# A chunked bidirectional recurrence: a masked copy over a prefilled negative identity, and another order of the work around it

## The chip, the cores and the metric

The kernel runs on one core of a Trainium2 chip. The metric is the device time of one execution in microseconds. It is shown as the median of three runs, and beside it one execution was taken with the hardware profiler.

## The reference

The program computes two model blocks, one after the other. The change lies in the second block, in its recurrence `wkv_scan`, which runs forward and backward over 1,280 tokens (256 of context, whose final states start the rest, then 1,024 of the sequence), with 8 heads of 64 columns:

```python
def wkv_scan(s0, r, w, k, v, a, b, reverse):
    def step(s, inp):
        r_t, w_t, k_t, v_t, a_t, b_t = inp
        sa = jnp.einsum('bhvk,bhk->bhv', s, a_t)
        s = s * w_t[:, :, None, :] + sa[..., :, None] * b_t[:, :, None, :] + v_t[..., :, None] * k_t[:, :, None, :]
        return s, jnp.einsum('bhvk,bhk->bhv', s, r_t)
```

It is called with `v` as it is, the decay as `w`, `-kk` as `a` and `kk * a` as `b`. Only the outputs of the sequence are used; of the context only the final states count.

## The kernel before, in words

`rwkv_chunks` (line 1974) computes the recurrence in `NCK` = 20 chunks of `CK` = 64 tokens, both directions at once (index `d`). Four of them are context. Within a chunk the step-by-step recurrence becomes a lower triangular system of 64 unknowns for each head and direction. Its matrix I + L is inverted by doubling: `x` holds the inverse of the diagonal blocks so far (of 2, 4, 8, ... tokens), and each of `LEVELS` = 5 levels makes blocks twice as large.

A level is a chain over three engines. TensorE multiplies `lm` (the lower matrix) by `x` in `products`, into PSUM tile `ps0`; VectorE masks the result to the level's blocks in `masked` (line 2212, into `t1`). Beside that TensorE transposes `x` in `x_turned`, and ScalarE copies the transpose to `xt` (line 2162). TensorE multiplies both in `advanced`, again into `ps0`, and VectorE adds that to `x` in VectorE's `advanced` (line 2218). At the last level TensorE forms the transposed result instead (line 2314, `rc_ps<-rc_xt,rc_t`), and VectorE adds it to `xt` (line 2288): the inverse.

Names of PSUM tiles are joined to `rc_ps` in the trace; a group is recognized by what it reads:

- `rc_x,rc_lm`: the product of a level (in the text P0 to P4); `all_ident,rc_x`: the transposes of x (four records); `rc_t,rc_xt`: the advance (A0 to A3). X0 to X3 are the updates of x on line 2218.
- `rc_ar,rc_bst` with 64x128 elements: the lower products of the next chunk (`lower`), from which VectorE makes `lm` (line 2224); `rc_bst,rc_ar`: the row product (`lower_rows`), from which `first` makes the start of `x`.
- `rc_ar,rc_kst`: the key product, from which VectorE makes `lk` (line 2267). `rc_v,rc_lk` and `rc_S,rc_ar`: the right side of the system (`right_side`, `right_side_of_state`); `rc_g,rc_xt` and `rc_gs,rc_xt`: `solved`; `rc_lm,rc_u`, `rc_lk,rc_v` and `rc_ar,rc_S`: `outputs` and `outputs_of_state`; `rc_u,rc_brows` and `rc_v,rc_krows`: `state`. `all_ident,rc_vst`: transposes of v.

The start of `x` for the next chunk is I - L on the first, smallest blocks:

```python
V.tensor_tensor(paired(b["x"][:, sl]), crossed(0, d), over(T.level[d][0][:]), ALU.mult)
V.tensor_tensor(paired(b["x"][:, sl]), paired(b["x"][:, sl]), over(T.ident2[:]), ALU.add)
```

These are lines 2230 and 2234, two instructions each (one per direction).

GpSimd forms the factors `bst`, `kst` and `ar` of the chunk after (lines 2092 to 2116) and copies v (line 2125). VectorE adds the outputs to `y` in `outputs` (lines 2244 and 2247, four instructions in a chunk), sums up the state in `summed` (line 2253) and scales it in `advance_state` (line 2260).

Each engine runs its own instructions strictly in the order in which `body` writes them down; semaphores hold an instruction until its operands are there. TensorE's order is written out for all 20 chunks, the other engines loop over the later ones two at a time. In `body(i)` TensorE works on the inverse of chunk i, and between its levels on the solution, the outputs and the state of chunk i - 1. Bodies 0 to 4 form no outputs. Double buffers are chosen by `sl`.

## Time and profile before

| | us |
|---|---|
| median of three runs | 3118.64 |
| lowest, highest | 3117.55, 3123.63 |
| the profiled execution | 3105.69 |
| its span in the profile | 3103.9 |
| TensorE matmuls busy | 2486.0 |
| VectorE busy | 1704.7 |
| ScalarE busy | 964.7 |
| GpSimd busy | 630.0 |

The profiled execution took 12.95 us less than the median of the three runs. The span begins with the first and ends with the last recorded instruction; 1.8 us of the execution lie around it. Busy time is a mean over stages that differ much: the recurrence is one stage of them, and only what its own rows say holds for it. TensorE works on 32-bit data in several passes, so the trace has two matmul records for each matmul of the program, and 32 records for a product. A timeline row joins neighbouring instructions of one kind: its first number is the start of the first, its second the time until the last one's result. In brackets stands how long the engine had idled, and on what it had waited; "issue" is a time in which it waited for nothing that the profile shows.

### The profile page before, as it was taken

The page shows a single profiled execution, that of the slowest core. Times are in us where ns is not written, and L with a number is a line of the kernel's source. Part 1 is how long each engine was busy: PE and PEld are TensorE (multiplying, and loading weights), DVE is VectorE, ACT ScalarE, POOL GpSimd, SP SyncE. Part 2 cuts the span into 40 slices and gives each one's busy share as a digit, 9 for nine tenths or more (in the row PEclk, how much of TensorE's full clock was granted, in tenths as well). Part 3 has the DMA queues.
Part 4 walks back from the last instruction along what each step waited for, and adds up shares of the span by engine and source line. Part 5 has one row for each costly group of instructions (what it writes and reads, how often), then busy time and mean ns, then how long its engine had stood idle before and what let it go on. Part 6 is the DMA issues. An engine that isn't in the chain of part 4 may idle for free. (4 is left out here: it accounts for less than half of the span.)

```text
span 3103.9 us, 57059 instructions
## 1 busy us (share of the span) xinstructions
PE 2486.0 (80%) x23774; PEld 1915.1 (62%) x23774; DVE 1704.7 (55%) x2130; ACT 964.7 (31%) x1492; POOL 630.0 (20%) x618
## 2 busy tenths in 40 slices
PE   4698998879989299997667777773575689999993
PEld 1586655447657278885256666661365678888882
DVE  2792448421124412664645555556435589999993
ACT  2111441210021400012333333320102067777772
POOL 0231457112200033220054444410000010001000
PEclk8899999989999599996589999996785589999997
DMA  9132004321122212110411011101434089999994
GB/s 379 71 126 87 1 1 146 92 102 34 51 85 85 86 58 68 41 35 16 170 28 26 20 24 24 24 4 48 166 104 176 0 326 409 398 399 389 398 385 151
DMA packets 132709, 405.57 MB, mean 131 GB/s; under 512 B 55082, under 2 KB 64938, under 8 KB 102674
## 3 DMA queue, kind: packets, MB, share of 16 engines
q1 hardware_dynamic: 119252, 359.52, 30.8%
q0 software_dynamic: 4608, 16.78, 2.2%
q10 hardware_dynamic: 8640, 26.19, 2.2%
q8 instruction: 168, 2.75, 0.4%
q14 instruction: 41, 0.34, 0.0%
HBM read 346.83 MB, written 55.61 MB: 130 GB/s over the span
## 5 line engine op out<-in xcount | busy, mean ns | idle before, releaser
L2927 DVE TENSOR_TENSOR ex_wl<-ew_raw,ex_wh 128x2048 fp32r<-128x2048 f32 x192 | 435.5, 2289 | 41.9 <-ACT ex_wh L2889 38.5
L2889 ACT ACTIVATE ex_wh<-ew_raw 128x2048 fp32r<-128x2048 f32 x192 | 367.5, 1919 | 217.0 <-PEq L89 109.3
L125 PE MATMUL sp_acc<-b2h_hi,sp_wh 128*128 128x512 f32 (+1 forms) x528 | 194.8, 369 | 11.8 <-POOL sp_wl L1614 11.8
L125 PE MATMUL sp_acc<-b2h_lo,sp_wh 128*128 128x512 f32 (+1 forms) x528 | 194.5, 368 | 0.0
L125 PE MATMUL sp_acc<-b2h_hi,sp_wl 128*128 128x512 f32 (+1 forms) x528 | 194.2, 368 | 0.0
L2162 ACT ACTIVATE rc_xt<-rc_ps 128x256 f32<-128x256 f32 x200 | 69.3, 391 | 229.1 <-PE rc_ps L2321 228.9
L2212 DVE TENSOR_TENSOR rc_t<-rc_ps,b_level 128x256 f32<-128x256 f32 x200 | 75.5, 419 | 103.4 <-PE rc_ps L2307 103.4
L1100 DVE TENSOR_TENSOR merge_sg<-b_pj,merge_sg 128x512 f32<-128x512 f32 x16 | 11.1, 692 | 217.8 <-ACT merge_sg L1086 217.8
L2810 POOL DMA_INDIRECT x<-ex_o,ex_at x16 | 26.5, 1656 | 490.8 <-DVE ex_o L2950 490.8
L125 PE MATMUL merge_acc<-merge_hh,merge_wh 128*128 128x512 f32 x256 | 101.5, 397 | 26.0 <-POOL merge_wl L119 20.7
L2798 POOL DMA_INDIRECT ex_xs<-h,ex_at x16 | 27.5, 1721 | 456.9 <-DVE ex_at L2952 434.2
L125 PEld LDWEIGHTS sp_acc<-b2h_hi,sp_wh 128*128 128x128 f32 x528 | 100.1, 190 | 28.6 <-POOL sp_wl L1614 12.2
L1612 POOL CAST sp_wh<-sp_w 128x1024 fp32r<-128x1024 f32 x26 | 27.1, 1042 | 434.8 <-DMA sp_w<-in_w_conv 251.2
L2307 PE MATMUL rc_ps<-rc_x,rc_lm 64*64 64x64 f32 x3200 | 73.5, 227 | 51.6 <-DVE rc_x L2234 50.0
L125 PEld LDWEIGHTS sp_acc<-b2h_hi,sp_wl 128*128 128x128 f32 x528 | 100.0, 189 | 16.7
L125 PEld LDWEIGHTS sp_acc<-b2h_lo,sp_wh 128*128 128x128 f32 x528 | 100.2, 190 | 16.4
L125 PE MATMUL pr_acc<-h_hi,pr_wh 128*128 128x512 f32 x224 | 89.6, 400 | 22.2 <-POOL pr_wl L205 20.6
L2831 PE MATMUL ex_G<-ex_wh,ex_xh 128*128 128x512 f32 x256 | 102.1, 399 | 1.4 <-DVE ex_xl L2932 1.4
L2307 PEld LDWEIGHTS rc_ps<-rc_x,rc_lm 64*64 64x64 f32 x3200 | 59.2, 136 | 68.1 <-issue 67.9
L2831 PE MATMUL ex_O<-ex_wh,ex_hh 128*128 128x512 f32 x256 | 99.7, 389 | 1.6 <-DVE ex_hl L2943 1.6
L2831 PE MATMUL ex_U<-ex_wh,ex_xh 128*128 128x512 f32 x256 | 100.9, 394 | 0.0
L2833 PE MATMUL ex_G<-ex_wh,ex_xl 128*128 128x512 f32 x256 | 100.7, 393 | 0.0
(459 smaller groups left out, 6379.3 us busy)
## 6 DMA issues: line engine op xcount, KB each, us to landing
ew_raw<-in_exp_gate SPq DMA_DIRECT2D x64, 1024.0 KB, 7.6
ew_raw<-in_exp_up SPq DMA_DIRECT2D x64, 1024.0 KB, 8.9
ew_raw<-in_exp_down SPq DMA_DIRECT2D x64, 1024.0 KB, 7.7
b_pj<-in_ada_w SPq DMA_DIRECT2D x24, 1024.0 KB, 18.4
rc_ac<-ac SPq DMA_DIRECT2D x40, 256.0 KB, 3.8
merge_w<-in_w_merge SPq DMA_DIRECT2D x16, 512.0 KB, 4.9
ac<-rp_ac SPq DMA_DIRECT2D x4, 2048.0 KB, 7.1
pr_w<-in_w_main SPq DMA_DIRECT2D x14, 512.0 KB
```

What stands on the lines that cost most here:

```text
L125: ins = nc.tensor.matmul(out, w[a][:, k, :], h[b][:, k, cols], start=(first and n == 0), stop=(last and n == 2))
L1100: nc.vector.tensor_tensor(sg[:, h, 0:1, :], merged[:, ds(b, 1), h * 512:(h + 1) * 512], sg[:, h, 0:1, :], ALU.mult).then_inc(weighed, 1)
L1612: nc.gpsimd.tensor_copy(wh[:, i % 2], w[:]).then_inc(q["w_rounded"], 1)
L2162: A.activation(dst(t[d]), src(d), ACT.Copy).then_inc(q[d][ready], 1)
L2212: V.tensor_tensor(paired(b["t1"][:]), crossed(0, d), over(T.level[d][l + 1][:]), ALU.mult).then_inc(s["t1_ready"], 1)
L2307: last = M(ps[n][c * CK:(c + 1) * CK, f, at:at + w], l(t[d])[k, h], r(t[d])[k, h], start=(i == 0), stop=(i == len(terms) - 1))
L2798: nc.gpsimd.indirect_dma_start(xs[:, m % 2, :], None, h_dram, bass.IndirectOffsetOnAxis(at[:, m:m + 1], 0)).then_inc(gathered[m % 2], 16)
L2810: nc.gpsimd.indirect_dma_start(x2, bass.IndirectOffsetOnAxis(at[:, x:x + 1], 0), o[:, x % 2, :], None, compute_op=ALU.add).then_inc(scatte ...
L2831: nc.tensor.matmul(acc[:, c], ah[:, k, :], wh[:, s, kk, c], start=(k == 0), stop=False)
L2833: last = nc.tensor.matmul(acc[:, c], al[:, k, :], wh[:, s, kk, c], start=False, stop=(k == KD - 1))
L2889: nc.scalar.activation(wh[:, n % RING], raw[:, n % RING], ACT.Copy).then_inc(q["w_hi"], 1)
L2927: V.tensor_tensor(wl[:, n % RING], raw[:, n % RING], wh[:, n % RING].bitcast(f32), ALU.subtract).then_inc(q["w_lo"], 1)
```

## The change

- VectorE's pair of multiplication and identity addition becomes one `copy_predicated` for each direction: where the mask of the first level is not zero it copies the row product over `x`, and elsewhere `x` stays. For that ScalarE fills `x` of the next chunk with minus the identity, between its third and fourth transposed copies. The first mask loses its sign. `x` now holds the negative of what it held; the updates on lines 2218 and 2288 become subtractions, and the solution is copied with the scale -1.
- TensorE: in the first level the transposes of x come ahead of `right_side`, and `right_side_of_state` and the advance ahead of the key product. `lower` of the next chunk moves ahead of the last level's transposes, and `lower_rows` ahead of its advance, with a wait for the last mask.
- VectorE: `lk` moves behind the first update of x, `outputs` ahead of the fourth mask, `summed` ahead of the fourth update, `lower` ahead of the last mask.

```diff
--- before.py
+++ after.py
...
@@ -2155,14 +2155,22 @@
                         hold(act, passed)
                         A.activation(b["e_end"][:, sl], b["last"], ACT.Copy).then_inc(s["kept"], 1)
 
-                def copy(done, count, dst, src, ready):
+                def copy(done, count, dst, src, ready, scale=1.0):
                     for d in range(2):
                         act.wait_ge(joint[done] if done in joint else q[d][done], count)
                         hold(act, passed)
-                        A.activation(dst(t[d]), src(d), ACT.Copy).then_inc(q[d][ready], 1)
+                        A.activation(dst(t[d]), src(d), ACT.Copy, scale=scale).then_inc(q[d][ready], 1)
 
                 def transposed(i, l, sl):
                     copy("xt_done", LEVELS * i + l + 1, lambda b: b["xt"][:, sl], lambda d: stayed(1, d), "xt_next")
+
+                def filled(c, sl):
+
+                    for d in range(2):
+                        if not (isinstance(c, int) and c < 2):
+                            act.wait_ge(joint["xi_done"], c - 1)
+                        hold(act, passed)
+                        A.activation(t[d]["x"][:, sl], spread(T.ident2[:], 1, HP), ACT.Copy, scale=-1.0).then_inc(q[d]["filled"], 1)
 
                 def right_side(count):
                     for d in range(2):
@@ -2180,7 +2188,7 @@
                         right_side(i)
                     transposed(i, 1, sl)
                     if old is not None:
-                        copy("u_done", i, lambda b: paired(b["u"][:]), lambda d: crossed(2, d), "u_ready")
+                        copy("u_done", i, lambda b: paired(b["u"][:]), lambda d: crossed(2, d), "u_ready", -1.0)
                     for d in range(2):
                         b, s = t[d], q[d]
                         act.wait_ge(s["rows_done"], i + 1)
@@ -2188,6 +2196,8 @@
                         A.activation(b["brows"][:, sl], stayed(3, d), ACT.Copy, scale=-1.0).then_inc(s["b_rows"], 1)
                         A.activation(b["krows"][:, sl], stayed(3, d, 1), ACT.Copy).then_inc(s["k_rows"], 1)
                     transposed(i, 2, sl)
+                    if following is not None:
+                        filled(i + 1, 1 - sl)
                     transposed(i, 3, sl)
                     transposed(i, 4, sl)
                     copy("v_done", i + 1, lambda b: b["v"][:], lambda d: stayed(3, d), "v_rows")
...
@@ -2215,7 +2226,7 @@
                     for d in range(2):
                         b, s = t[d], q[d]
                         dve.wait_ge(joint["xp_done"], (LEVELS - 1) * i + l + 1)
-                        V.tensor_tensor(paired(b["x"][:, sl]), crossed(0, d), paired(b["x"][:, sl]), ALU.add).then_inc(s["x_next"], 1)
+                        V.tensor_tensor(paired(b["x"][:, sl]), paired(b["x"][:, sl]), crossed(0, d), ALU.subtract).then_inc(s["x_next"], 1)
 
                 def lower(c, sl):
                     for d in range(2):
@@ -2227,11 +2238,9 @@
                     for d in range(2):
                         b, s = t[d], q[d]
                         dve.wait_ge(joint["pl_done"], c + 1)
-                        V.tensor_tensor(paired(b["x"][:, sl]), crossed(0, d), over(T.level[d][0][:]), ALU.mult).then_inc(s["x_ready"], 1)
-                    for d in range(2):
-                        b, s = t[d], q[d]
-                        dve.wait_ge(s["x_ready"], 2 * c + 1)
-                        V.tensor_tensor(paired(b["x"][:, sl]), paired(b["x"][:, sl]), over(T.ident2[:]), ALU.add).then_inc(s["x_ready"], 1)
+                        dve.wait_ge(s["filled"], c + 1)
+                        hold(dve, passed)
+                        V.copy_predicated(paired(b["x"][:, sl]), over(T.level[d][0][:].bitcast(u32)), crossed(0, d)).then_inc(s["x_ready"], 1)
 
                 def outputs(c):
                     for d in range(2):
@@ -2261,31 +2270,32 @@
 
                 def body(i, sl, half, old, here, following):
                     masked(i, 0)
+                    advanced(i, 0, sl)
                     for d in range(2):
                         b, s = t[d], q[d]
                         dve.wait_ge(joint["pk_done"], i + 1)
                         V.tensor_tensor(paired(b["lk"][:, sl]), crossed(3, d, 2 * CK), over(T.plus[d][:]), ALU.mult).then_inc(s["lk_ready"], 1)
-                    advanced(i, 0, sl)
                     masked(i, 1)
                     advanced(i, 1, sl)
                     masked(i, 2)
                     advanced(i, 2, sl)
-                    masked(i, 3)
                     if old == "all":
                         outputs(i - 1)
-                    advanced(i, 3, sl)
+                    masked(i, 3)
                     if old is not None:
                         summed(i)
+                    advanced(i, 3, sl)
+                    if following is not None:
+                        lower(i + 1, 1 - sl)
                     masked(i, 4)
                     if old is not None:
                         advance_state(1 - sl, i)
                     if following is not None:
-                        lower(i + 1, 1 - sl)
                         first(i + 1, 1 - sl)
                     for d in range(2):
                         b, s = t[d], q[d]
                         dve.wait_ge(joint["xi_done"], i + 1)
-                        V.tensor_tensor(b["xt"][:, sl], stayed(1, d), b["xt"][:, sl], ALU.add).then_inc(s["inverse"], 1)
+                        V.tensor_tensor(b["xt"][:, sl], b["xt"][:, sl], stayed(1, d), ALU.subtract).then_inc(s["inverse"], 1)
 
                 dve.wait_ge(cleared, 5)
                 lower(0, 0)
@@ -2327,13 +2337,16 @@
                     crossing(2, 2 * CK, (lambda b: b["bst"][:, sl], lambda b: b["ar"][:, sl])).then_inc(joint["pm_done"], 1)
 
                 def lower_rows(c, sl):
+                    if c:
+                        for d in range(2):
+                            pe.wait_ge(q[d]["t1_ready"], LEVELS * c)
                     crossing(0, CK, (lambda b: b["ar"][:, sl, :, 0:CK], lambda b: b["bst"][:, sl])).then_inc(joint["pl_done"], 1)
 
                 def products(i, l, sl):
                     for d in range(2):
                         if l == 0:
                             pe.wait_ge(q[d]["lm_ready"], i + 1)
-                            pe.wait_ge(q[d]["x_ready"], 2 * i + 2)
+                            pe.wait_ge(q[d]["x_ready"], i + 1)
                         else:
                             pe.wait_ge(q[d]["x_next"], (LEVELS - 1) * i + l)
                     crossing(0, CK, (lambda b: b["lm"][:, sl, :, 0:CK], lambda b: b["x"][:, sl])).then_inc(joint["t1_done"], 1)
@@ -2341,7 +2354,7 @@
                 def x_turned(i, l, sl):
                     for d in range(2):
                         if l == 0:
-                            pe.wait_ge(q[d]["x_ready"], 2 * i + 2)
+                            pe.wait_ge(q[d]["x_ready"], i + 1)
                             if i:
                                 pe.wait_ge(q[d]["inverse"], i)
                         else:
@@ -2394,15 +2407,14 @@
 
                 def body(i, sl, old, following):
                     products(i, 0, sl)
+                    x_turned(i, 0, sl)
                     if old is not None:
                         right_side(i, 1 - sl)
-                    x_turned(i, 0, sl)
+                        right_side_of_state(i, 1 - sl)
+                    advanced(i, 0, sl)
                     for d in range(2):
                         pe.wait_ge(q[d]["stk"], i + 1)
                     crossing(3, 2 * CK, (lambda b: b["kst"][:, sl], lambda b: b["ar"][:, sl])).then_inc(joint["pk_done"], 1)
-                    if old is not None:
-                        right_side_of_state(i, 1 - sl)
-                    advanced(i, 0, sl)
                     x_turned(i, 1, sl)
                     products(i, 1, sl)
                     if old is not None:
@@ -2427,14 +2439,14 @@
                     if old is not None:
                         state(i, 1 - sl)
                     advanced(i, 3, sl)
-                    x_turned(i, 4, sl)
-                    products(i, 4, sl)
                     if following:
                         if old == "all":
                             for d in range(2):
 
                                 pe.wait_ge(q[d]["y_added"], 2 * (i - CTX_CK) + 1)
                         lower(i + 1, 1 - sl)
+                    x_turned(i, 4, sl)
+                    products(i, 4, sl)
                     for d in range(2):
                         s = q[d]
                         if old is not None:
@@ -2446,9 +2458,9 @@
                         pe.wait_ge(s["v_staged"], i + 1)
                     for d in range(2):
                         turned(stayed(3, d), t[d]["vst"]).then_inc(q[d]["v_done"], 1)
-                    advanced(i, 4, sl)
                     if following:
                         lower_rows(i + 1, 1 - sl)
+                    advanced(i, 4, sl)
 
                 lower(0, 0)
                 lower_rows(0, 0)
@@ -3156,7 +3168,6 @@
     low = np.stack([(r // (2 * n) == c // (2 * n)) & (r // n > c // n) for n in (1, 2, 4, 8, 16, 32)]).astype(f)
     high = np.stack([(r // (2 * n) == c // (2 * n)) & (r // n < c // n) for n in (1, 2, 4, 8, 16, 32)]).astype(f)
     out["levels"] = np.stack([low, high])
-    out["levels"][:, 0] *= -1
     return {n: np.ascontiguousarray(a) for n, a in out.items()}
```

On TensorE, the start of a body that has outputs (P0 to the first transposes of the second level), before:

```order
L2307 MATMUL rc_ps<-rc_x,rc_lm 64x64 x16
L2307 MATMUL rc_ps<-rc_v,rc_lk 64x64 x16
L2321 MATMUL rc_ps<-all_ident,rc_x 128x128 x4
L2307 MATMUL rc_ps<-rc_ar,rc_kst 64x128 x16
L2314 MATMUL rc_ps<-rc_S,rc_ar 64x64 x16
L2307 MATMUL rc_ps<-rc_t,rc_xt 64x64 x16
L2321 MATMUL rc_ps<-all_ident,rc_x 128x128 x4
```

and now (line numbers are ten higher in the changed kernel):

```order
L2317 MATMUL rc_ps<-rc_x,rc_lm 64x64 x16
L2331 MATMUL rc_ps<-all_ident,rc_x 128x128 x4
L2317 MATMUL rc_ps<-rc_v,rc_lk 64x64 x16
L2324 MATMUL rc_ps<-rc_S,rc_ar 64x64 x16
L2317 MATMUL rc_ps<-rc_t,rc_xt 64x64 x16
L2317 MATMUL rc_ps<-rc_ar,rc_kst 64x128 x16
L2331 MATMUL rc_ps<-all_ident,rc_x 128x128 x4
```

The key product has moved from ahead of the first advance to behind it.

On TensorE, the end of such a body and the next chunk's first product, before:

```order
L2307 MATMUL rc_ps<-rc_t,rc_xt 64x64 x16
L2321 MATMUL rc_ps<-all_ident,rc_x 128x128 x4
L2307 MATMUL rc_ps<-rc_x,rc_lm 64x64 x16
L2307 MATMUL rc_ps<-rc_ar,rc_bst 64x128 x16
L2321 MATMUL rc_ps<-all_ident,rc_vst 128x128 x4
L2314 MATMUL rc_ps<-rc_xt,rc_t 64x64 x16
L2307 MATMUL rc_ps<-rc_bst,rc_ar 64x64 x16
L2307 MATMUL rc_ps<-rc_x,rc_lm 64x64 x16
```

and now:

```order
L2317 MATMUL rc_ps<-rc_t,rc_xt 64x64 x16
L2317 MATMUL rc_ps<-rc_ar,rc_bst 64x128 x16
L2331 MATMUL rc_ps<-all_ident,rc_x 128x128 x4
L2317 MATMUL rc_ps<-rc_x,rc_lm 64x64 x16
L2331 MATMUL rc_ps<-all_ident,rc_vst 128x128 x4
L2317 MATMUL rc_ps<-rc_bst,rc_ar 64x64 x16
L2324 MATMUL rc_ps<-rc_xt,rc_t 64x64 x16
L2317 MATMUL rc_ps<-rc_x,rc_lm 64x64 x16
```

The lower products stand ahead of the last transposes, and the row product ahead of the last advance.

On VectorE, the same stretch from the third update of x on, before:

```order
L2218 TENSOR_TENSOR rc_x<-rc_ps,rc_x 128x256 x2
...
L2212 TENSOR_TENSOR rc_t<-rc_ps,b_level 128x256 x2
...
L2244 TENSOR_TENSOR b2p_y<-rc_ps,b2p_y 128x4x64
...
L2247 TENSOR_TENSOR b2p_y<-rc_ps,b2p_y 128x4x64
...
L2218 TENSOR_TENSOR rc_x<-rc_ps,rc_x 128x256 x2
L2253 TENSOR_TENSOR rc_sum<-rc_ps,rc_S 128x256 x2
...
L2212 TENSOR_TENSOR rc_t<-rc_ps,b_level 128x256 x2
L2260 TENSOR_TENSOR rc_S<-rc_sum,rc_e_end 128x256 x2
...
L2224 TENSOR_TENSOR rc_lm<-rc_ps,b_minus 128x512 x2
L2230 TENSOR_TENSOR rc_x<-rc_ps,b_level 128x256 x2
...
L2234 TENSOR_TENSOR rc_x<-rc_x,b_ident 128x256 x2
L2288 TENSOR_TENSOR rc_xt<-rc_ps,rc_xt 128x256 x2
```

and now:

```order
L2229 TENSOR_TENSOR rc_x<-rc_x,rc_ps 128x256 x2
...
L2253 TENSOR_TENSOR b2p_y<-rc_ps,b2p_y 128x4x64
...
L2256 TENSOR_TENSOR b2p_y<-rc_ps,b2p_y 128x4x64
...
L2223 TENSOR_TENSOR rc_t<-rc_ps,b_level 128x256 x2
L2262 TENSOR_TENSOR rc_sum<-rc_ps,rc_S 128x256 x2
...
L2229 TENSOR_TENSOR rc_x<-rc_x,rc_ps 128x256 x2
...
L2235 TENSOR_TENSOR rc_lm<-rc_ps,b_minus 128x512 x2
...
L2223 TENSOR_TENSOR rc_t<-rc_ps,b_level 128x256 x2
L2269 TENSOR_TENSOR rc_S<-rc_sum,rc_e_end 128x256 x2
L2243 COPY_PREDICATED rc_x<-b_level,rc_ps 128x256 x2
L2298 TENSOR_TENSOR rc_xt<-rc_xt,rc_ps 128x256 x2
```

The output additions stand ahead of the fourth mask, the `lm` pair ahead of the last one, and one pair of masked copies stands where two pairs stood.

## Rows read from the trace of the kernel before

**Rows 1.** The page, its costliest groups: busy, mean ns, idle before and its releaser.

```profile
L2307 PE MATMUL rc_ps<-rc_x,rc_lm 64*64 64x64 f32 x3200 | 73.5, 227 | 51.6 <-DVE rc_x L2234 50.0
```

**Rows 2.** Windows, recurrence: us, busy PE, PEld, DVE, ACT, POOL, clock, DMA.

```profile
1562.00:2092.00 530.00, 402.62 (x14243) 347.67 (x14244) 293.02 (x696) 170.77 (x554) 221.79 (x345) 0.96 0.09 21
```

**Rows 3.** Timeline of DVE: start, us, line, op, count; three of twenty identity additions.

```profile
1566.71 1.35 DVE L2234 TENSOR_TENSOR rc_x<-rc_x,b_ident 128x256 f32<-128x256 f32 x2
...
1686.53 1.74 DVE L2234 TENSOR_TENSOR rc_x<-rc_x,b_ident 128x256 f32<-128x256 f32 x2
...
2060.80 0.75 DVE L2234 TENSOR_TENSOR rc_x<-rc_x,b_ident 128x256 f32<-128x256 f32 x2
```

**Rows 4.** Timeline of PE, one body without visible stalls.

```profile
1929.22 0.69 PE L2307 MATMUL rc_ps<-rc_x,rc_lm 64*64 64x64 f32 x32 [2.42 <-DVE rc_x L2234]
...
1930.90 1.10 PE L2307 MATMUL rc_ps<-rc_ar,rc_kst 64*64 64x128 f32 x32
...
1931.82 1.04 PE L2314 MATMUL rc_ps<-rc_S,rc_ar 64*64 64x64 f32 x30
...
1933.92 0.77 PE L2321 MATMUL rc_ps<-all_ident,rc_x 128*128 128x128 f32 x4 [0.53 <-DVE rc_x L2218]
...
1940.76 1.13 PE L2314 MATMUL rc_ps<-rc_ar,rc_S 64*64 64x64 f32 x32
...
1944.19 0.69 PE L2307 MATMUL rc_ps<-rc_t,rc_xt 64*64 64x64 f32 x32
...
1946.95 0.69 PE L2307 MATMUL rc_ps<-rc_x,rc_lm 64*64 64x64 f32 x32
...
1947.46 1.05 PE L2307 MATMUL rc_ps<-rc_ar,rc_bst 64*64 64x128 f32 x32
...
1949.04 1.09 PE L2314 MATMUL rc_ps<-rc_xt,rc_t 64*64 64x64 f32 x30
...
1950.02 0.63 PE L2307 MATMUL rc_ps<-rc_bst,rc_ar 64*64 64x64 f32 x30
...
1953.25 0.69 PE L2307 MATMUL rc_ps<-rc_x,rc_lm 64*64 64x64 f32 x32 [2.60 <-DVE rc_x L2234]
```

**Rows 5.** Timeline of DVE, the same body.

```profile
1932.08 1.29 DVE L2267 TENSOR_TENSOR rc_lk<-rc_ps,b_plus 128x512 f32<-128x512 f32 x2 [1.33 <-PE rc_ps L2307]
...
1943.18 0.76 DVE L2212 TENSOR_TENSOR rc_t<-rc_ps,b_level 128x256 f32<-128x256 f32 x2 [1.38 <-PE rc_ps L2307]
...
1945.78 0.75 DVE L2218 TENSOR_TENSOR rc_x<-rc_ps,rc_x 128x256 f32<-128x256 f32 x2
...
1947.72 0.76 DVE L2212 TENSOR_TENSOR rc_t<-rc_ps,b_level 128x256 f32<-128x256 f32 x2 [0.54 <-PE rc_ps L2307]
...
1948.39 0.75 DVE L2260 TENSOR_TENSOR rc_S<-rc_sum,rc_e_end 128x256 f32<-128x256 f32 x2
...
1950.70 0.76 DVE L2230 TENSOR_TENSOR rc_x<-rc_ps,b_level 128x256 f32<-128x256 f32 x2 [0.36 <-PE rc_ps L2307]
```

**Rows 6.** Timeline of POOL, the same body.

```profile
1942.21 1.33 POOL L2116 TENSOR_TENSOR rc_ar<-b2p_pT,rc_e 128x256 f32<-128x256 f32 x2 [3.12 <-PE rc_ps L2314]
...
1949.16 0.74 POOL L2125 COPY rc_vst<-b2p_pT 128x256 f32 x2 [5.61 <-PE rc_ps L2321]
```

**Rows 7.** Instructions of line 2234: ns min/median/max.

```profile
L2234 DVE TENSOR_TENSOR rc_x<-rc_x,b_ident x40: 416/831/985, 1566.7 to 2061.1; 128x256 f32<-128x256 f32 x40
```

**Rows 8.** Instructions of line 2517: ns min/median/max.

```profile
L2517 DVE RECIPROCAL ro_t<-ro_t x8: 3352/3353/3354, 2112.7 to 2189.6; 128x512 f32<-128x512 f32 x8
```

**Rows 9.** Timeline of ACT, between its third and fourth transposed copy.

```profile
1942.38 0.66 ACT L2162 ACTIVATE rc_xt<-rc_ps 128x256 f32<-128x256 f32 x2 [2.81 <-PE rc_ps L2321]
```

**Rows 10.** Timeline of PE, a body with stalls.

```profile
2017.67 0.27 PE L2307 MATMUL rc_ps<-rc_gs,rc_xt 64*64 64x64 f32 x1 [1.69 <-issue]
...
2021.97 0.21 PE L2307 MATMUL rc_ps<-rc_lk,rc_v 64*64 64x64 f32 x1 [0.59 <-issue]
```

**Rows 11.** DMA queues from 1686.53 to 2060.80: packets, MB, share.

```profile
q8 instruction: 83, 1.36, 1.5%
```

More of the change, by code:

```diff
@@ L1981, in rwkv_chunks @@
         ka = ph.sb("ka", [P, 2, HP])
-        names = ("decays", "kept", "stk", "v_staged", "rows_done", "v_done", "lm_ready", "x_ready",
+        names = ("decays", "kept", "stk", "v_staged", "rows_done", "v_done", "lm_ready", "filled", "x_ready",
                  "lk_ready", "b_rows", "k_rows", "v_rows", "t1_ready", "xt_done", "xt_next", "x_next", "inverse",
@@ L2198, in _ @@
                 decays(0, 0, 0)
+                filled(0, 0)
                 keep(0, 0)
@@ L2201, in _ @@
                 right_side(NCK)
-                copy("u_done", NCK, lambda b: paired(b["u"][:]), lambda d: crossed(2, d), "u_ready")
+                copy("u_done", NCK, lambda b: paired(b["u"][:]), lambda d: crossed(2, d), "u_ready", -1.0)
             @block.vector
```

## The prediction

> **What bounds the kernel now.** I read the page first. Its group of the recurrence's row products names the wait that matters: before those 3,200 matmuls TensorE sat idle for 51.6 us, nearly all of it until the identity addition on line 2234 had run [rows 1]. That is twenty waits of 2.5 us, one for each chunk. The windows view then gives the size of the stage: 530 us, in which TensorE's matmuls are busy 403 us, VectorE 293 us and everything else less, at a granted clock of 0.96 of the 2.4 GHz level [rows 2]. No engine is full; the stage is a chain that goes to and fro between TensorE and VectorE.
>
> The VectorE timeline gives the period. The identity addition comes at 1566.71 us (chunk 0), 1686.53 (chunk 5) and 2060.80 (chunk 19) [rows 3]. So bodies 0 to 4 take (1686.53 - 1566.71) / 5 = 23.96 us each, and bodies 5 to 18, which also form outputs, (2060.80 - 1686.53) / 14 = 26.73 us. One of the latter shows no stall of TensorE's own: 1929.22 to 1953.25, 24.03 us [rows 4]. I use it as the skeleton; the other 2.7 us are stalls that the views call "issue", such as 1.69 and 0.59 us in the middle of runs of matmuls that wait for nobody [rows 10].
>
> In the skeleton the reader should see three things. From the last but one advance (A3, 1944.19) to the next chunk's first product it takes 9.06 us, with two idle spots of TensorE in it, the last 2.60 us long [rows 4]. X3, VectorE's update of x after A3, starts at 1945.78, though A3's 0.69 us of data had ended at 1944.88: four output additions stood ahead of it [rows 4, 5]. And the end of the chunk is serial: row product (1950.02), mask (1950.70), identity addition, which takes 1.74 us for two instructions, next product (1953.25) [rows 3 to 5].
>
> **The change, part by part.**
>
> *Start of a body.* The key product (1930.90, 0.92 us until the next group at 1931.82) now stands behind the first advance instead of ahead of it [rows 4]. The advance and X0 come 0.92 us earlier; TensorE is then busy with the key product until about when X0's first half is ready, so the next transposes start 0.7 us earlier, not 0.9. The lk pair (1.29 us) moves behind X0; it ends as the next product does, and costs 0.1 us at most [rows 5]. I take 0.7 us.
>
> *Outputs ahead of the fourth mask.* They read what the group at 1940.76 writes, complete 1.13 us later, 1941.89 [rows 4]. With the 0.7 us it is 1941.2. Four output additions lasted 1.9 us (from the end of the mask pair, 1943.94, less its overlap, to 1945.78), so the mask, which would have been ready at 1942.5, starts at 1943.15 [rows 5]. In bodies 5 to 18 A3 therefore stays where it was: the 0.7 us are spent here. What is bought is that X3 no longer waits for the outputs.
>
> *From A3 on, with A3 at 0.* X3 starts at 0.8. The new chunk's lower products (0.98 us of issue, 1947.46 to the next group) fit on TensorE under X3. P4 follows X3 by 1.17 us as it does now (1945.78 to 1946.95): 2.0. The lm pair, as long as lk, 1.29 us, now comes ahead of the last mask and ends near 2.9; the mask would have been possible at 2.77 (P4 to mask is 0.77 us now), so it starts at 2.9. The row product is new ahead of the last advance and must wait for that mask, since both use one PSUM tile; mask to product is 1.01 us at A3 (1943.18 to 1944.19), so it starts at 3.9 and its data end at 4.55. The masked copy follows at 4.6. The identity additions are gone. Two copies at 0.76 us the pair and 0.15 us to the product: next body at 5.5, against 9.06 [rows 4, 5]. The advance itself (0.98 us of issue) lies behind the row product and is done by 5.4, beside the copy.
>
> *A price in the other direction.* The v copy on GpSimd starts right after the v transposes, at 1949.16 now [rows 6]; these come earlier against the S update, which so far ran alone: two in 0.75 us [rows 5]. The identity addition, with two SBUF inputs as the S update has, shows what GpSimd's work beside it does: median 831 ns, minimum 416, and 0.75 us for both in the last chunk, where GpSimd had nothing left [rows 3, 7]. At that price S ends 1.0 us later, and the copy with it by 0.7. I take half, 0.35 us: 5.85. The Trainium skill says the same of this pair (SBUF — State Buffer, "Who interferes with whom": a VectorE instruction with two SBUF inputs contends with a GpSimd instruction that reads SBUF). It counts inputs, and the masked copy has one in SBUF (the mask), so by it that copy is free of GpSimd; with its old destination read as well it would not be.
>
> *The masked copy's own price.* No row shows this operation. Below, a PSUM operand with a mask from SBUF costs 0.38 us each [rows 5]. Above, the dearest elementwise row is the reciprocal, 3,353 ns for 512 columns, so 1.68 us for 256 [rows 8]. I take 0.38, the row nearest in operands, size and work.
>
> *At nothing:* two fills of x on ScalarE, some 0.7 us a body, lie in its 2.81 us of idling before the fourth transposed copy [rows 9]; subtractions for additions and scales of -1 change no shape. TensorE now waits for GpSimd's ar at A3 + 0.5, so 1944.7; the pair ends at 1943.5 and earlier now [rows 6], so nothing queues there.
>
> *Sum.* Bodies 5 to 18: 9.06 - 5.85 = 3.2 us. Bodies 0 to 4 have no outputs: they keep the 0.7, and their X3 was 0.8 earlier already, so 0.7 + (8.3 - 5.85) = 3.15. Nineteen hand-overs at 3.2 are 61 us; body 19 gives nothing that counts. Against this stand the stalls. In bodies 5 to 18 83 instruction packets of 16 KB came, 5.9 a body [rows 11], or one for some 241 of a body's 1,424 matmuls and weight loads (14,243 and 14,244 of them over twenty bodies [rows 2]); the two stalls shown lie about that many apart. Those that fall into a wait, such as the 2.6 us, are free today; most of that wait goes. I put 0.5 us a body on it: -9.5. The page Runtime: NRT & Kernel Launch of the Trainium skill, "Instruction fetch mechanics", calls such a crossing mostly hidden; by that nothing is taken off and the gain is 61. The trace does not agree, with 2.7 us a body over the skeleton. Total 51.5 us of the profiled 3105.69, so 3054 there; the median of the runs is 3118.64, and the forecast on it is **3067 us**.
>
> **The rivals.**
>
> *A. Instruction supply takes half.* If each packet needs about 4.1 us from one to the next, 5.9 of them make 24.2 us, whatever the chain does. For it: stalls come in series 4.3 us apart [rows 10]. Against: the skeleton shows 24.03 us without any. Bodies 5 to 18 gain 2.5, less what the series costs elsewhere, some 1.2 in all; 19 x 1.3 = 25: 3093 us.
>
> *B. The masked copy is dear; slower.* At 1.68 us, and held up by GpSimd as line 2234 is (831 over 375 ns, +0.45), each is 1.75 us dearer than I take it, the pair 3.5 us, against a net gain of 2.7: 19 x 0.8 = 15 us slower, 3134. It decides from 1.35 us above my price per instruction, 1.7 us. Against it: nothing else that reads PSUM and a mask here costs over 0.42 us for 256 columns.
>
> *C. It does not do what it says.* If the row product waits for more than the last mask, the serial end comes back in another order: no change, 3119. Nothing in the program's order shows such a wait.
>
> **How the numbers follow.** Forecast 0.78, A 0.15, B 0.04, C 0.03. Own range of the forecast: down to 3046, with no loss to GpSimd (0.35 x 19 = 7) and no added stalls (9.5) and a few us more where fewer crossings meet waits; up to 3082 with S fully blocked (0.35 x 19 = 7) and the copy at 0.6 (8). Taking in A: 3045 to 3097. A difference of 0.2% (6 us) is about what a measurement of this kernel can tell from none. Faster 0.91: the forecast, A but for its worst part; same 0.05; slower 0.04.
>
> **What would show it.** Right: the period between masked copies near 24 us in the late chunks and 21 in the early ones; 5.5 to 6.2 us from A3 to the next product; TensorE's wait before it under 0.6 us; masked copies near 0.4 us; S updates between 0.4 and 0.8 us each; about as many "issue" stalls as before or more. Wrong: masked copies above 0.8 us; a wait of TensorE for GpSimd's ar; the A3 product later than 15.0 us after the body's start because the outputs hold the fourth mask longer than 0.7 us; packet spacing near 4.1 us with TensorE stalled at each.

## The result and the profile after

The changed kernel takes 3075.32 us (median of 4 runs, 3072.97 to 3077.50), the kernel before 3118.10 us in the runs beside it. The ratio is 0.9865, with a 95% interval of 0.9842 to 0.9888: 43 us faster. The profiled execution took 3077.50 us with a span of 3075.7 us. The one profiled before was faster than all four of these, 12.4 us under the median, so the two profiles stand only 28 us apart; medians are compared where the sum matters, and the profiles for what happened in a body. Of the executions of all runs below one, of e1, took 5113.43 us; it is left out, and e1's median is that of its other three.

The windows view of the recurrence in the changed kernel (us, then busy PE, PEld, DVE, ACT, POOL, granted clock, share and GB/s of DMA):

```profile
1562.00:2062.00 500.00, 407.86 (x14250) 350.76 (x14252) 271.05 (x656) 184.10 (x592) 223.82 (x346) 0.97 0.10 23
```

It answers to [rows 2]: 30 us shorter in this profile, with the same number of matmuls and about the same mean clock. The VectorE timeline has the masked copies where the identity additions of [rows 3] were: chunks 0, 5 and 19.

```profile
1566.20 0.76 DVE L2243 COPY_PREDICATED rc_x<-b_level,rc_ps 128x256 f32<-128x256 uint32 x2
...
1682.96 0.77 DVE L2243 COPY_PREDICATED rc_x<-b_level,rc_ps 128x256 f32<-128x256 uint32 x2
...
2028.81 0.77 DVE L2243 COPY_PREDICATED rc_x<-b_level,rc_ps 128x256 f32<-128x256 uint32 x2
```

Bodies 0 to 4 take (1682.96 - 1566.20) / 5 = 23.35 us (before: 23.96), bodies 5 to 18 (2028.81 - 1682.96) / 14 = 24.70 us (before: 26.73). By these the early bodies gained 3 us in all and the late ones 28.

The mean clock hides a difference in the early bodies. The windows view over bodies 0 to 4, before and then after:

```profile
1566.71:1686.53 119.82, 87.04 (x3008) 73.64 (x3008) 65.58 (x155) 41.48 (x134) 55.98 (x89) 0.97 0.11 25
```

```profile
1566.20:1682.96 116.76, 92.85 (x2991) 78.61 (x2993) 59.71 (x146) 43.25 (x139) 55.56 (x87) 0.92 0.12 26
```

For as many matmuls TensorE was busy 5.8 us longer, with a granted clock of 0.92 where it was 0.97; only part of that need lie on the chain. In the late bodies it is the other way round, a little: 0.99 after, 0.96 before.

The instructions of the new copy and of the S update, with minimum, median and maximum in ns:

```profile
L2243 DVE COPY_PREDICATED rc_x<-b_level,rc_ps x40: 430/440/458, 1566.2 to 2029.2; 128x256 f32<-128x256 uint32 x40
```

```profile
L2269 DVE TENSOR_TENSOR rc_S<-rc_sum,rc_e_end x38: 412/568/650, 1610.9 to 2052.7; 128x256 f32<-128x256 f32 x38
```

The masked copy costs 0.44 us, where 0.38 was taken. The S update, 0.416 us before (the median of line 2260 in that trace), now has a median of 0.568. The timelines of one body show why; first TensorE, from the product of one body to that of the next (it answers to [rows 4]):

```profile
1982.39 0.69 PE L2317 MATMUL rc_ps<-rc_x,rc_lm 64*64 64x64 f32 x32 [0.22 <-DVE rc_x L2243]
...
1984.49 1.09 PE L2324 MATMUL rc_ps<-rc_S,rc_ar 64*64 64x64 f32 x30 [0.19 <-PE rc_ps L2317]
...
1987.49 0.69 PE L2317 MATMUL rc_ps<-rc_x,rc_lm 64*64 64x64 f32 x32
...
1993.89 1.12 PE L2324 MATMUL rc_ps<-rc_ar,rc_S 64*64 64x64 f32 x32
...
1995.52 0.69 PE L2317 MATMUL rc_ps<-rc_x,rc_lm 64*64 64x64 f32 x32
...
1998.34 0.69 PE L2317 MATMUL rc_ps<-rc_t,rc_xt 64*64 64x64 f32 x32
...
2001.04 0.43 PE L2317 MATMUL rc_ps<-rc_ar,rc_bst 64*64 64x128 f32 x3 [1.13 <-issue]
...
2003.67 0.69 PE L2317 MATMUL rc_ps<-rc_bst,rc_ar 64*64 64x64 f32 x32 [0.40 <-DVE rc_t L2223]
...
2005.51 0.73 PE L2317 MATMUL rc_ps<-rc_x,rc_lm 64*64 64x64 f32 x32 [0.22 <-DVE rc_x L2243]
```

then VectorE:

```profile
1995.42 0.42 DVE L2253 TENSOR_TENSOR b2p_y<-rc_ps,b2p_y 128x256 f32 x1 [0.50 <-PE rc_ps L2324]
...
1997.34 0.74 DVE L2223 TENSOR_TENSOR rc_t<-rc_ps,b_level 128x256 f32<-128x256 f32 x2
...
2003.44 1.07 DVE L2269 TENSOR_TENSOR rc_S<-rc_sum,rc_e_end 128x256 f32<-128x256 f32 x2
...
2004.58 0.78 DVE L2243 COPY_PREDICATED rc_x<-b_level,rc_ps 128x256 f32<-128x256 uint32 x2
```

and GpSimd:

```profile
2003.30 0.94 POOL L2125 COPY rc_vst<-b2p_pT 128x256 f32 x2 [6.64 <-PE rc_ps L2331]
```

The pair of S updates takes 1.07 us beside GpSimd's pair of copies, where it took 0.75 [rows 5], and the copies take 0.94 where they took 0.74 [rows 6]: both are longer where they overlap. TensorE's wait for the start of x has shrunk from 2.6 to 0.22 us. But the fourth mask starts at 1997.34, 1.82 us after its product began (1995.52), and not 0.77 as between the last product and its mask in [rows 4, 5]: the output additions, from 1995.42, stand ahead of it. And in the middle of the lower products TensorE stalls 1.13 us for nothing that the profile shows.

Those stalls are the other half of the picture. The waits view of 1562 to 2062 us, TensorE's main rows inside the recurrence (total us, times, longest), before:

```profile
PE rc_ps L2307 <- DVE rc_x L2234: 50.0, 20, 2.7
PE rc_ps L2321 <- DVE rc_x L2218: 30.1, 43, 1.4
PE rc_ps L2307 <- issue: 26.0, 54, 1.7
PE rc_ps L2307 <- DVE rc_t L2212: 7.7, 7, 1.1
PE rc_ps L2314 <- issue: 2.2, 3, 0.9
PE rc_ps L2321 <- issue: 1.5, 2, 0.9
```

and after:

```profile
PE rc_ps L2317 <- issue: 46.2, 75, 2.2
PE rc_ps L2317 <- DVE rc_t L2223: 21.2, 34, 1.2
PE rc_ps L2317 <- DVE rc_x L2243: 5.1, 18, 1.4
PE rc_ps L2331 <- issue: 3.8, 5, 1.1
PE rc_ps L2331 <- DVE rc_x L2229: 3.3, 6, 0.6
PE rc_ps L2324 <- issue: 2.5, 3, 1.0
```

45 us of waiting for the start of x are gone (50.0 to 5.1), and 27 us of the transposes' waiting for the updates of x (30.1 to 3.3), since the key product and the lower products now fill those places. Against these 72 us the "issue" stalls rose from 29.7 to 52.5 us, and the waits for the masks from 7.7 to 21.2: half of what was gained came back, 23 us of it as stalls.

The stalls can be tied to instruction packets. The trace records when each packet of queue q8 starts. Of the changed kernel's 83 idle spots that are called "issue" (52.5 us) 69 end 2.2 to 3.0 us after such a packet began, with 48.5 us; of the 59 before (29.7 us) it is 36, with 24.2 us. Of the other rows of TensorE's timeline about a quarter start so after the change, and 0.18 before. The packets are never closer than 3.35 us.

### The profile page after: what moved, and what is told of

The parts are those of the page before. It is cut to its first block and busy times, and to the rows that moved or that the text cites. A ratio compares the mean times of both kernels' runs of the same rounds, so it can differ in the third digit from the quotient of the medians.

```text
span 3075.7 us, 57144 instructions
## 1 busy us (share of the span) xinstructions
PE 2491.9 (81%) x23774; PEld 1918.4 (62%) x23774; DVE 1682.3 (55%) x2090; ACT 978.1 (32%) x1532; POOL 627.9 (20%) x618
## 5 line engine op out<-in xcount | busy, mean ns | idle before, releaser
L2229 DVE TENSOR_TENSOR rc_x<-rc_x,rc_ps 128x256 f32<-128x256 f32 x160 | 60.1, 417 | 116.2 <-PE rc_ps L2317 116.0
L125 PE MATMUL pr_acc<-h_hi,pr_wh 128*128 128x512 f32 x224 | 89.6, 400 | 22.6 <-POOL pr_wl L205 20.5
L125 PE MATMUL merge_acc<-merge_hl,merge_wh 128*128 128x512 f32 x256 | 100.6, 393 | 0.0
L125 PE MATMUL merge_acc<-merge_hh,merge_wl 128*128 128x512 f32 x256 | 100.4, 392 | 0.0
```

The source lines that it names most:

```text
L125: ins = nc.tensor.matmul(out, w[a][:, k, :], h[b][:, k, cols], start=(first and n == 0), stop=(last and n == 2))
```

## The experiments

The forecast's theory was a chain of dependent steps plus a modest price for each packet of TensorE instructions (the chain theory). Its rival A held that the supply of TensorE's instructions is the brake itself. Twelve kernels were run, in three groups, each beside the kernel before on the same chip. In the cuts of code some operands are shortened (`x` for `paired(b["x"][:, sl])` and the like).

### The two halves of the change: e1, e2

e1 is the kernel before with the masked copy:

```diff
-V.tensor_tensor(x, crossed(0, d), level0, ALU.mult)
-V.tensor_tensor(x, x, ident2, ALU.add)
+V.copy_predicated(x, level0, crossed(0, d))
```

(with ScalarE's fill and the changed signs). e2 is the changed kernel with those two lines back, and every order as changed.

> The order of before, with the masked copy, the fills on ScalarE and the changed signs. The pair of masked copies takes 0.78 us where multiplication and identity addition took 2.4, so the next body's first product can come 1.6 us earlier. Chain theory (the period is a chain, stalls of instruction supply cost some 0.5 us a crossing on top): 19 x 1.6 = 31 us, less 0.3 us a body for crossings that the wait used to hide: 25 us faster than before, TensorE's wait for the start of x about 1 us. Supply theory (a packet of TensorE instructions each 4.2 us or so is a floor): late bodies are held at 25 us, 15 to 25 us faster. Rival of the result: if the reordering did all of the gain, under 5 us faster.

> The order of the changed kernel, with multiplication and identity addition on VectorE as before. The last stretch then has 0.75 to 1.7 us more ahead of the next body's first product. Chain theory: 19 x 1.4 = 27 us slower than the changed kernel, so 15 to 20 us faster than before. Supply theory: the extra wait hides stalls, 5 to 15 us slower than the changed kernel. If the order is worth nothing (0.7 us gained at the start and given back to the outputs): level with before plus or minus 6 us.

Measured: e1 3082.25 us, ratio 0.9869 (0.9851 to 0.9887). e2 3093.89 us, ratio 0.9912 (0.9897 to 0.9927). By the medians beside them (3121.99) that is 40 us for the masked copy alone and 28 us for the order alone. Together they give 43, not 68; by the ratios the masked copy alone can't be told from the whole change. The two halves shorten the same bodies, and something else holds them. By the profiles a late body takes 25.63 us in e1 and 25.46 in e2, but e1's is of its slowest execution of the three (3093.66 us). The supply theory's 15 to 25 us for e1 was too little, the chain theory's 25 too; 40 is even more than the 31 us that the shorter chain was worth, and no run shows why. e2 is 19 us slower than the changed kernel, outside the supply theory's 5 to 15 and short of the chain theory's 27.

### Fewer instructions on TensorE: e4, e8, e9, e10

e4 is the changed kernel without three of the terms that TensorE sums up: the state's part of the right side in the solution, the v part of the outputs, the v part of the state.

```diff
-crossing(2, CK, (xt, g), (xt, gs))
+crossing(2, CK, (xt, g))
...
-crossing(2, CK, (u, lm), (v, lk))
+crossing(2, CK, (u, lm))
...
-crossing(3, CK, (brows, u), (krows, v))
+crossing(3, CK, (brows, u))
```

> The changed kernel without the second term of the solution, of the outputs and of the state (gs, v with lk, v with krows left out): 192 of TensorE's 1,424 matmuls and weight loads a body go, and all lie where TensorE waits for VectorE anyway, so the chain between the levels is as long as before (the state's and the outputs' groups end before the mask they stand beside). Chain theory with 0.5 us a crossing: 0.75 crossings fewer a body, 0.4 us, 7 us faster than the changed kernel. Supply theory (about 4.2 us from packet to packet): 0.75 x 4.2 = 3.1 us a body, bounded by the chain of 21.8 us: 35 to 45 us faster than the changed kernel, and the late period near 22 us.

Measured: 3036.70 us, ratio 0.9729 (0.9713 to 0.9746): 39 us faster than the changed kernel, against 7 by the chain theory. Three rows of TensorE's timeline show a body of e4 without a stall on the chain (one of 0.23 us falls into a wait for the mask):

```profile
1856.19 0.69 PE L2317 MATMUL rc_ps<-rc_x,rc_lm 64*64 64x64 f32 x32
...
1871.91 0.69 PE L2317 MATMUL rc_ps<-rc_t,rc_xt 64*64 64x64 f32 x32 [1.09 <-DVE rc_t L2223]
...
1877.85 0.69 PE L2317 MATMUL rc_ps<-rc_x,rc_lm 64*64 64x64 f32 x32 [0.26 <-DVE rc_x L2243]
```

15.72 us to A3, 21.66 to the next product. That is the chain of the changed kernel, laid bare; the changed kernel's own late bodies are 3.0 us above it (24.70). The waits view of e4, in the same window, says where its 39 us came from:

```profile
PE rc_ps L2317 <- DVE rc_t L2223: 53.0, 71, 1.6
PE rc_ps L2317 <- issue: 15.1, 31, 1.8
PE rc_ps L2324 <- issue: 1.5, 3, 0.7
PE rc_ps L2331 <- issue: 0.8, 1, 0.8
```

The stalls fell from 52.5 to 17.4 us, and TensorE's waits for the masks rose from 21.2 to 53.0: now the chain shows.

But e4 also took TensorE's work away, not its instructions alone. e10 puts the time back in another form, three matmuls of 128 columns ahead of each shortened group, which nobody reads:

```diff
+for _ in range(3):
+    M(ps[n][0:CK, 0, 0:2 * CK], l[0:CK, 0], r[0:CK, 0:2], start=True, stop=True)
 crossing(n, CK, ...)
```

> e4 (three terms left out), with TensorE's time put back in another form: ahead of the solution, the outputs and the state stand three matmuls of 128 columns each, whose result nobody uses. They keep TensorE busy about as long as the 16 small ones did (some 0.6 us each place), with 36 instead of 192 matmuls and weight loads a body. If it is the number of instructions that brakes, the time is e4's: 3035 to 3045 us. If it is TensorE's busy time in those places, it is the changed kernel's: 3070 to 3080.

Measured: 3041.28 us, ratio 0.9748 (0.9727 to 0.9769). Windows of e4 and of e10 over their recurrence (columns as above):

```profile
1562.00:2024.00 462.00, 370.51 (x12512) 317.92 (x12512) 271.99 (x660) 183.79 (x592) 225.15 (x347) 0.98 0.11 24
```

```profile
1567.00:2030.00 463.00, 403.05 (x12842) 351.34 (x12842) 271.17 (x659) 183.81 (x592) 224.16 (x346) 0.98 0.11 24
```

e10 keeps TensorE's matmuls busy 403 us and its weight loads 351, as long as the changed kernel (408 and 351), and yet takes 5 us more than e4 and 34 less than the changed kernel, with 12,842 matmul records in place of 14,250. The granted clock is no rival here: 0.97 in the changed kernel's row, 0.98 in these two. So TensorE's busy time is not what brakes; the number of its instructions is, or the small form of the 192 that were left out, since number and form changed together. For the number speaks the tie of the stalls to the packets: in e10 all 25 idle spots that are called "issue" in the same window (13.1 us, from 52.5) end 2.2 to 3.0 us after a packet began. This is the run that settles the theories' main point.

e8 is the kernel before with e4's cut, e9 is e1 with it.

> The kernel before, with the same three terms left out as in e4 (192 of 1,424 matmuls and weight loads a body). If instruction supply was already the brake before, the late period falls from 26.7 to the chain's 24.0 and the early one from 24.0 to 23: 14 x 2.5 + 5 x 1 = 40 us faster than before. If a crossing only costs some 0.5 us, 7 us faster.

> e1 (masked copy, order of before) with the same terms left out. With most of the supply's brake off, the orders can be compared as chains: that of before with the masked copy takes 24.0 - 1.6 = 22.4 us a late body, the changed one 21.8. Supply theory: the late period is 22.9 to 23.4, the total 5 to 15 us above e4's, and 25 to 30 us below e8's. Had the order some value of its own beyond the chain, e4 would be ahead by over 20 us; had it none, they would be level.

Measured: e8 3096.90 us, ratio 0.9921 (0.9903 to 0.9939), 24 us under the kernel before, between the 40 and the 7 that were expected; e9 3069.19 us, ratio 0.9826 (0.9808 to 0.9845). The brake was there before the change and cost less: the same cut brings 24 us before, 13 with the masked copy alone (e1 to e9) and 39 now. And with the brake eased the order is worth more than expected: from e9 to e4 32 us (5 to 15 were expected), from e1 to the changed kernel 7. Of the 32, 8 us (14 x 0.6) were written down as the difference of the late chains (22.4 and 21.8 us a body); by the profiles the late bodies of e9 and e4 are 24.21 and 22.77 us, the early ones 23.78 and 21.24, so the late bodies make 20 us of the difference and the early ones 13. The order's worth was underrated in both, and part of the difference is the granted clock: 0.97 in e9's late bodies and 1.00 in e4's, 0.85 and 0.95 in the early ones, where TensorE was busy 92.7 us in e9 and 84.9 in e4 for the same matmuls.

### Shorter chain at the same number of instructions: e5, e3

e5 leaves out VectorE's four output additions.

```diff
-V.tensor_tensor(paired(yv), crossed(2, d), paired(yv), ALU.add).then_inc(s["y_added"], 1)
+dve.sem_inc(s["y_added"], 1)
...
-V.tensor_tensor(yv, stayed(2, d, 1), yv, ALU.add).then_inc(s["y_added"], 1)
+dve.sem_inc(s["y_added"], 1)
```

> The changed kernel without VectorE's four output additions a body (their semaphores still rise). The fourth mask then need not wait for them: from P3 to A3 1.8 us instead of 2.8. Chain theory: 15 bodies x 1.0 = 15 us faster than the changed kernel. Supply theory: TensorE then stalls for instructions in their place, 0 to 4 us faster.

Measured: 3076.63 us, ratio 0.9853 (0.9838 to 0.9869), level with the changed kernel. The place did get shorter: product and advance around the fourth mask are 1.79 us apart (1898.43 to 1900.22), where the changed kernel has 2.82.

```profile
1898.43 0.69 PE L2317 MATMUL rc_ps<-rc_x,rc_lm 64*64 64x64 f32 x32
...
1900.22 0.53 PE L2317 MATMUL rc_ps<-rc_t,rc_xt 64*64 64x64 f32 x18
```

A microsecond was taken off this place in 15 bodies, and the late bodies are as long as they were (24.80 us). Of the 15 us TensorE's waits for the masks show 7 gone (21.2 to 13.8), while the stalls rose by 3 (to 55.9); and in the late bodies its granted clock was 0.97 where the changed kernel had 0.99, and its busy time 4.7 us longer. So the stalls took only part of it. It is still the chain theory's clearest defeat: none of the forecast 15 us is in the median.

e3 puts the right side ahead of the first transposes again:

```diff
-x_turned(i, 0, sl)
 if old is not None:
     right_side(i, 1 - sl)
+x_turned(i, 0, sl)
+if old is not None:
     right_side_of_state(i, 1 - sl)
```

> The changed kernel with the right side ahead of the first transposes, as before the change. In the changed kernel 0.89 us lie from the right side to that of the state, where 0.60 were its issue before. The first advance should start at 2.5 to 2.7 us after the body's start instead of 2.98. Supply theory: taken up by stalls, as the outputs' 1.0 us were in e5: 0 to 3 us. Chain theory: 19 x 0.35, 6 to 7 us faster.

Measured: 3078.10 us, ratio 0.9873 (0.9850 to 0.9896): nothing. In its trace the first advance starts at 2.56 us after the body's first product, as said:

```profile
1879.29 0.69 PE L2317 MATMUL rc_ps<-rc_x,rc_lm 64*64 64x64 f32 x32 [0.20 <-DVE rc_x L2243]
...
1881.95 0.63 PE L2317 MATMUL rc_ps<-rc_t,rc_xt 64*64 64x64 f32 x29
```

(the second row is the advance's main part; its first two records come at 1881.85). So the step shows where the missing 0.4 us of the forecast's first term went, and again a shorter chain bought no time: 0 to 3 us were the supply theory's, 6 to 7 the chain theory's, and e3's executions span 7 us, so of the two only the latter is made unlikely.

### More instructions: e7, inconclusive

```diff
+def more(n=14):
+    for _ in range(n):
+        pe.sem_inc(passed, 1)
```

`more()` stands ahead of TensorE's waits in its advances and in its transposes from the second level on.

> The changed kernel with 126 semaphore increments a body more on TensorE (nobody waits for them), 14 ahead of each of nine waits; they are 0.49 of a packet. Supply theory: 0.49 x 4.2 = 2.1 us a body, 35 to 45 us slower than the changed kernel, and the packets at the same spacing. Chain theory: 0.25 us a body for the crossing and a little for issue, 5 to 15 us slower.

Measured: 3321.33 us, ratio 1.0649 (1.0627 to 1.0670), 246 us slower than the changed kernel, far more than either theory says. The increments themselves are the cost:

```profile
1744.46 1.15 PE L2324 MATMUL rc_ps<-rc_S,rc_ar 64*64 64x64 f32 x32 [0.19 <-PE rc_ps L2317]
...
1747.18 0.69 PE L2317 MATMUL rc_ps<-rc_t,rc_xt 64*64 64x64 f32 x32 [1.57 <-issue]
```

Between these two groups lie 2.72 us, 0.88 in the changed kernel: 1.84 us for 14 increments, 0.13 us each. 126 of them are 16 us a body, part of it hidden. What the instructions' fetching adds can't be told from that. The stalls here are not those of the other runs: only 16 of 113 "issue" spots end 2.2 to 3.0 us after a packet began.

### Versions that compute everything: e6, e11, e12

e6 has VectorE add the two halves of the right side, so that TensorE needs 64 instructions fewer in a body.

```diff
-crossing(2, CK, (xt, g), (xt, gs))
+crossing(2, CK, (xt, g))
...
+V.tensor_tensor(b["g"][:], b["g"][:], stayed(2, d, 1), ALU.add).then_inc(s["g_ready"], 1)
```

e11 has these additions behind the second mask, the transposes of the factors ahead of the second advance and the solution behind it. e12 is e11 with e3's step.

> The changed kernel with the whole reference computed, but VectorE adds the two halves of the right side (two additions a body, ahead of lk) in place of TensorE's second term and ScalarE's second copy: 64 of 1,424 TensorE instructions fewer, a quarter of a packet, and VectorE's second mask 0.8 us later. Supply theory: 0.25 x 4.2 = 1.05 us a body, 15 to 20 us faster than the changed kernel. Chain theory: 0.8 us a body later, 10 to 15 us slower.

> The whole reference. e6, with VectorE's two additions behind the second mask instead of ahead of it, the transposes of the factors ahead of the second advance, the solution behind it, and ScalarE's copies in that order. The chain should be the changed kernel's 21.8 us again and not 0.8 longer, with 64 TensorE instructions fewer a body. Supply theory: a third of e4's gain of 39 us, 10 to 15 us faster than the changed kernel, 3060 to 3067. If the supply did not matter: level with the changed kernel.

> e11 with the right side ahead of the first transposes again, as before the change: the state's right side waits for the first half's last result, and the transposes would fill that gap of 0.3 us. Chain: 0.3 to 0.45 us a body shorter. With instruction supply still the brake 0 to 4 us of it are seen, without it 6 to 8.

Measured: e6 3071.44 us (ratio 0.9841, 0.9821 to 0.9860), e11 3072.69 (0.9853, 0.9834 to 0.9871), e12 3071.68 (0.9850, 0.9831 to 0.9868). All three lie 3 to 4 us under the changed kernel by their medians, and by their intervals none can be told from it. They are also no slower, though e6 was expected to lengthen the chain by 0.8 us. But 64 instructions fewer did not give a third of what 192 fewer give. The stalls fell a little (44 to 45 us in the same window, from 52.5), those of e4 to 17. The supply theory in the form "so many microseconds for each packet" does not predict that. By the profiles the late bodies take 24.63 us in e6 and 24.89 in e11 (24.70 in the changed kernel), the early ones 22.11 and 22.48 (23.35): what there is of a gain lies in the bodies without outputs.

## Why the prediction was right, and where it was off

Forecast 3067 us, measured 3075, with 43 us of the 51.5. The direction held, and so did the waits that the change was to remove. What the stalls take back was put far too low, and that the total came within 8 us is in part luck: the sum was made from the bodies of one profile, and by the two profiles the bodies gained 31 us, not 51.5. The rest of the 43 lies in the fast execution that was profiled before.

- **Start of a body, 0.7 us.** Measured 0.3: the second level's product comes at 5.10 us (1982.39 to 1987.49), after 5.40 before. The sum moved the key product away and did not see what else it had covered. `right_side_of_state` waits until the last result of `right_side` is there; in the changed kernel the two are neighbours, and a gap opens ("0.19 <-PE" in the row of 1984.49). e3 fills it and gets the forecast's A0 (2.56 against 2.51).
- **Outputs ahead of the fourth mask, A3 where it was (15.0 us).** Measured 15.95 in the body shown and 15.72 in e4's. 0.4 of this is the first miss handed on. Another 0.4 is a term that the sum put at nothing: the first addition starts 0.41 us after the data of the group that it reads (1993.89 + 1.12 = 1995.01; 1995.42). The last 0.2 in the body shown is a stall ahead of it. So the price of this step was right in kind (it spends what the start gains) and 0.75 us short in size, and an A3 later than 15.0 us was one of the forecast's own signs of being wrong. In e5 the bodies are no shorter without it.
- **From A3 to the next product, 5.85 us.** Measured in e4 5.94 (1871.91 to 1877.85), in the changed kernel 5.84, in a body without a stall there:

```profile
1878.36 0.93 PE L2317 MATMUL rc_ps<-rc_t,rc_xt 64*64 64x64 f32 x32 [1.11 <-DVE rc_t L2223]
...
1884.20 0.69 PE L2317 MATMUL rc_ps<-rc_x,rc_lm 64*64 64x64 f32 x32 [0.20 <-DVE rc_x L2243]
```

  Its parts held too: masked copy near the low bound (0.44, taken 0.38), S update half held up by GpSimd (0.57 between 0.42 and 0.83). The S update, with two SBUF inputs, became longer beside GpSimd; the masked copy, with its mask alone from SBUF, stayed within 430 to 458 ns. The rule of the Trainium skill that was weighed there (SBUF — State Buffer, "Who interferes with whom") fits both.
- **Stalls, 0.5 us a body more.** Late bodies: 24.70 - 21.7 = 3.0 us over a body without stalls on its chain, where it was 2.7: 0.3 more. Early bodies: e4's shortest takes 20.5 us from product to product, and 23.35 - 20.5 = 2.9; before, with 22.9 us the shortest, it was 23.96 - 22.9 = 1.0: 1.9 more. The early bodies gained 0.6 us and not 2.65. This is the term that failed most in size, and it is not of stalls alone: the early bodies also had the lower granted clock (0.92 after 0.97), with TensorE busy 1.2 us a body longer. The sum had no term for the clock. The stalls were taken as a price per crossing; by the waits views they rise where other waits shrink.
- **Packets.** The forecast's other sign, packets near 4.1 us apart with TensorE stalled at each, came half true: in the late bodies 83 packets come in 345.85 us, one each 4.17 us, and 53 of the 83 have a stall that ends 2.2 to 3.0 us after their start. Before it was 33 of 83, in e4 28 of 72. And e10 buys 34 us by fewer instructions at equal busy time. The Trainium skill calls such a crossing mostly hidden (Runtime: NRT & Kernel Launch, "Instruction fetch mechanics"); these rows do not agree.

By the profiles: five early bodies at 0.6 and fourteen late at 2.0 make 31 us, and the forecast's 51.5 less 2.0 x 5 = 10 of the early bodies (2.65 forecast, 0.6 measured), less 0.7 x 14 = 10 of the late ones (2.7 and 2.0), is 31.5. The medians moved by 43, as the profiled execution of before was a fast one; in which stage it was faster no trace shows.

Rival A got a chance of 0.15 and the time 3093. Its mechanism, supply as a brake, is the one that the runs bear out. Its floor of 24.2 us a late body is near the measured mean of 24.70, but it is no floor: single bodies take down to 22.8 us, and packets come as close as 3.35 us. Its 25 us stand nearer to the 31 of the profiles than the forecast's 51.5; the medians' 43 stand nearer to the forecast. B fell by one row (0.44 us, not 1.7), C by the trace.

What stays open: how the supply works. Fewer instructions in the solution alone (e11) gave next to nothing, fewer in the solution, the outputs and the state gave 39 us. It may be the dense stretches and not their total (the state's 64 matmuls, with as many weight loads, start between 1997.28 and 1998.25 us): over the late bodies a packet each 4.17 us is slower than the 3.35 at which the closest came. That is not shown; no run separated the three places. How much of the early bodies' loss is the clock is open too.

## What to carry to other kernels

When the sum of a chain is made, ask of each instruction that is moved away what else it was hiding: a result that its neighbour waits for counts as soon as the two stand side by side. When an engine shows stalls without a releaser ahead of a change that shortens its waits, expect them to take part of the gain, and try fewer and wider instructions there before shortening the chain further. Here 192 instructions fewer a body told and 64 fewer did not. Two edits that give 40 and 28 us alone gave 43 together; run them apart before adding them up. And before a difference of two profiles is put down to an order or a stall, compare the granted clock of the same stretches.

## What the runs showed of the hardware that was not expected

- TensorE's instructions can bind by their number (or their small form) while its time does not: at 403 us of busy matmuls e10 is 34 us faster than the changed kernel at 408, and 69 of the changed kernel's 83 "issue" stalls end 2.2 to 3.0 us after an instruction packet began.
- A semaphore increment in TensorE's own stream takes 0.13 us (e7, 14 of them 1.84 us).
- `copy_predicated` on 128x256 32-bit elements with the data in PSUM and the mask in SBUF takes 0.44 us, hardly more than the multiplication that it replaces (0.42), and stays within 430 to 458 ns with GpSimd's work beside it.
